# First norm's shift and scale formed on TensorE in column groups, weights loaded by rows

## The reference, cut to what matters

```
mod = c @ w_ada + b_ada                       # 1024 x 6144 weights, 25 MB
sh1, sc1, g1, sh2, sc2, g2 = split(mod, 6)
h    = rms_norm(x, g) * (1 + sc1) + sh1
proj = h @ w_in                               # 1024 x 3080: conv gates | z | xBC | dt (8 columns)
y_a  = short_conv(...); y_b = ssd(...)        # dt = softplus(dt_raw + bias) feeds the decay terms
x    = x + g1 * (concat(y_a, y_b) @ w_out)
h    = rms_norm(x) * (1 + sc2) + sh2
x    = x + g2 * moe(h)                        # 64 experts, top 8, 3 MB of weights each, plus a shared one
out  = rms_norm(x)
```

## Time and profile before

| | |
|---|---|
| three runs, median (lowest to highest) | 707.49 us (707.42 to 708.46) |
| the profiled execution: its time, its span | 708.67 us, 706.9 us |
| PE busy, DVE busy, ACT busy | 642.9, 293.1, 130.7 us |
| DMA, mean over the span | 355 GB/s |

### The profile page before, as it was taken

How to read it: one execution, slowest core, us unless ns; L and a number is a source line. 1 busy time by engine, 2 the same in 40 slices (tenths; PEclk the granted TensorE clock), 3 DMA queues, 4 the chain that set the end, 5 groups by cost and what they waited for, 6 DMA issues and landing times.

```text
span 706.9 us, 11349 instructions
## 1 busy us (share of the span) xinstructions
PE 642.9 (91%) x4206; PEld 374.9 (53%) x4206; DVE 293.1 (41%) x775; ACT 130.7 (18%) x278; POOL 43.4 (6%) x223
## 2 busy tenths in 40 slices
PE   0469999999998899999999999999999999997882
PEld 0448886854544555556545565455554555553440
DVE  4649996778274233231332313323233232331115
ACT  3501123031320111111111111111111111111112
POOL 7000000000201000000000000000000000000000
PEclk9999999999999999999999999999999999999997
DMA  7998699724029999999999999999999999999951
GB/s 232 395 386 313 246 353 373 292 108 178 1 86 424 420 421 421 419 421 420 420 421 418 423 420 420 422 420 422 420 419 420 420 420 420 421 420 420 420 228 61
DMA packets 46010, 250.72 MB, mean 355 GB/s; under 512 B 4673, under 2 KB 7809, under 8 KB 20993
## 3 DMA queue, kind: packets, MB, share of 16 engines
q1 hardware_dynamic: 44434, 248.59, 86.6%
q10 hardware_dynamic: 1520, 1.39, 0.6%
HBM read 248.91 MB, written 1.05 MB: 354 GB/s over the span
## 4 chain that ended last, share of the span: by engine, by line
PE 67%; DVE 17%; DMA 12%; issue 1%; ACT 1%; ACTq 1%; SPq 0%; DVEq 0%
PE PS L1529 10%; PE PS L1525 9%; PE PS L1535 9%; PE PS L1508 8%; DVE MOD L871 7%; DMA ring<-in_we_up_dram 7%; PE PS L1583 5%; DMA ring<-in_w_ada_dram 5%; PE PS L1561 5%; PE PS L1557 5%; PE PS L1566 4%; PE PS L1579 2%; PE PS L1544 2%; PE PS L1325 1%; PE PS L1471 1%
## 5 line engine op out<-in xcount | busy, mean ns | idle before, releaser
L1167 DVE SCALAR_TENSOR_TENSOR arena<-arena,gate,PS 128x128 f32<-128x128 f32 (+1 forms) x48 | 17.9, 373 | 176.6 <-ACT arena L786 176.6
L1529 PE MATMUL PS<-ring,arena 128*64 128x256 f32 x736 | 88.4, 391 | 0.0
L1325 PE MATMUL PS<-hT,ring 128*128 128x256 f32 x384 | 84.8, 380 | 0.0
L1325 PEld LDWEIGHTS PS<-hT,ring 128*128 128x128 f32 x384 | 72.5, 190 | 11.1 <-issue 1.6
L1178 DVE TENSOR_TENSOR YLO<-PS,YHI 128x512 fp32r<-128x512 f32 x57 | 39.4, 691 | 93.3 <-ACT YHI L797 93.3
L871 DVE SCALAR_TENSOR_TENSOR MOD<-ring,ccol,MOD 128x768 f32<-128x768 f32 (+2 forms) x72 | 66.9, 930 | 13.1 <-ACT MOD L664 6.7
L1535 PE MATMUL PS<-ring,arena 128*32 128x256 f32 x1024 | 64.4, 403 | 7.5 <-DMA ring<-in_we_up_dram 7.5
L1508 PE MATMUL PS<-G,H2HI 128*128 128x256 f32 (+1 forms) x256 | 69.5, 307 | 1.3 <-ACT arena L777 0.7
L1525 PE MATMUL PS<-ring,arena 128*128 128x512 f32 x144 | 66.4, 612 | 0.6 <-issue 0.6
L1529 PEld LDWEIGHTS PS<-ring,arena 128*64 128x64 f32 x736 | 49.6, 134 | 31.7 <-issue 2.1
L797 ACT CAST YHI<-PS 128x512 fp32r<-128x512 f32 x57 | 33.5, 587 | 169.3 <-PE PS L1561 79.7
(11 more groups left out here) (255 smaller groups left out, 623.5 us busy)
## 6 DMA issues: line engine op xcount, KB each, us to landing
ring<-in_we_gate_dram SPq DMA_DIRECT2D x64, 1024.0 KB, 18.1
ring<-in_we_up_dram SPq DMA_DIRECT2D x64, 1024.0 KB, 20.7
ring<-in_we_down_dram SPq DMA_DIRECT2D x64, 1024.0 KB, 19.3
ring<-in_w_ada_dram SPq DMA_DIRECT2D x5, 3072.0 KB, 11.4
ring<-in_w_in_dram SPq DMA_DIRECT2D x3, 3072.0 KB, 18.0
ring<-in_w_ada_dram SPq DMA_DIRECT2D x4, 1536.0 KB, 15.8
ring<-in_w_out_dram SPq DMA_DIRECT2D x1, 3072.0 KB, 18.7
ring<-in_w_ada_dram SPq DMA_DIRECT2D x1, 2048.0 KB, 26.0
```

What stands on the lines that cost most here:

```text
L1325: mm = pe.matmul(PS[:, 2 + q % QB, 0:TOK], w[:, k, (m % 6) * P:(m % 6) * P + P], hT[:, k, :], start=(k == 0), stop=(k == KD - 1))
L1529: m = pe.matmul(PS[64 * c:64 * c + 64, 6, 0:FE].rearrange("p (a n) -> p a n", a=2), xt[:, k, :], gu_cols(w[0], k, c), start=(k == 0), stop ...
```

## The change

- The first 2048 columns of `w_ada` come in three pieces by rows (3, 3 and 2 of the 8 row groups, all 2048 columns, `ADA_K`), and PE forms c times them itself (`ada_rows`): per row group four matmuls, one for each group of 32 array columns, each with c repeated 32 times as weights and 512 columns moving. DVE adds the bias once (`mod1`), and four matmuls turn the result into columns. DVE's `ada(0)`, `ada(1)` and `ada(2)` are gone.
- The other 4096 columns come in six pieces, again 2048 columns wide and 3, 3 and 2 row groups; DVE's `ada(3)` to `ada(8)` do one instruction of 2048 columns per row group. One piece more stands in `LOADS`, and `w_in` piece 2 now stands ahead of the first of these six.
- `mod_rows` 0 to 3 need three of the six pieces, rows 4 to 7 all six. Rows 4 and 5 move behind group (0, 0) of the out projection.
- Applying `AB1` to `hT` is shared: even k on DVE, odd k on ACT. The dt matmuls use four column groups; a matmul with `lastcols` sums the groups and picks the eight dt columns.
- The bias is no longer copied by ACT from a row in the ring: four broadcasts of 64 KB and one row of 16 KB are loaded on ACT's queue. ACT's loads of the router weights and gains (WR, gffn, gfin, 1.25 MB) now stand behind its part of `hT`.

```diff
-LOADS = [(A, 0, 0), (A, 1, 1), (A, 2, 2), (I, 3, 3), (A, 3, 1), (I, 2, 0), (A, 4, 2), (I, 1, 1), (A, 5, 2),
-         (I, 0, 3), (A, 6, 2), (O, 0, 0), (S, 0, 1), (A, 7, 2), (O, 1, 3)]
+LOADS = [(A, 0, 0), (A, 1, 1), (A, 2, 2), (I, 3, 3), (I, 2, 0), (A, 3, 1), (A, 4, 2), (I, 1, 1), (A, 5, 2),
+         (I, 0, 3), (A, 6, 2), (O, 0, 0), (A, 7, 2), (S, 0, 1), (A, 8, 2), (O, 1, 3)]
+ADA_COLS = 2 * D
+ADA_K = [(0, 3), (3, 6), (6, 8)]
@@ def _(sp):
-                    user[s] = (ada_acc, nada)
+                    user[s] = (ada_used, j + 1) if j < 3 else (ada_acc, j - 2)
+                    c0, (k0, k1) = ADA_COLS * (j // 3), ADA_K[j % 3]
+                    sp.dma_start(ada_w(n), w_ada[0, :, c0:c0 + ADA_COLS].rearrange("(p k) n -> p k n", p=P)[:, k0:k1, :]
+                                 ).then_inc(loaded[s], 16)
@@ def _(act):
+            for g in range(4):
+                act.dma_start(bias1[32 * g:32 * g + 32, :],
+                              b_ada[0, 512 * g:512 * g + 512].partition_broadcast(32)).then_inc(bias1_in, 16)
+            act.wait_ge(mod_zero, 1)
+            act.dma_start(MOD[0:1, 2 * D:6 * D], b_ada[0:1, 2 * D:6 * D]).then_inc(bada_in, 16)
...
+            act.wait_ge(ab1_ready, 1)
+            act.wait_ge(xnT_ready, 4)
+            for k in range(1, KD, 2):
+                act.activation(hT[:, k, :], hT[:, k, :], ACT.Identity, bias=AB1[:, KD + k:KD + k + 1],
+                               scale=AB1[:, k:k + 1]).then_inc(h1_odd, 1)
@@ def _(dve):
+                k0, k1 = ADA_K[j % 3]
+                dve.wait_ge(loaded[slot_of(n)], loaded_count(n))
+                dst = MOD[:, ADA_COLS * (j // 3):ADA_COLS * (j // 3) + ADA_COLS]
+                for k in range(k0, k1):
+                    ins = dve.scalar_tensor_tensor(out=dst, in0=w[:, k - k0, :], scalar=ccol[:, k:k + 1], in1=dst,
+                                                   op0=ALU.mult, op1=ALU.add)
+                    link(ins, ada_acc if k == k1 - 1 else None)
...
+            dve.wait_ge(ada_used, 3)
+            dve.tensor_tensor(mod1, bank(1), bias1, ALU.add).then_inc(mod1_ready, 1)
...
-            ada(2)
             ada(3)
+            ada(4)
             for b in CONVS[0:3]:
                 conv(b)
-            ada(4)
+            ada(5)
@@ def _(pe):
+            def ada_rows(part_no):
+                n = load_no(A, part_no)
...
+                for k in range(k0, k1):
+                    for g in range(4):
+                        m = pe.matmul(PS[32 * g:32 * g + 32, 1, :], ccol[:, k:k + 1].to_broadcast([P, 32]),
+                                      ada_w(n)[:, k - k0, 512 * g:512 * g + 512], start=(k == 0), stop=(k == KD - 1))
+                m.then_inc(ada_used, 1)
...
+            for q in range(4):
+                m = pe.matmul(PS[:, 0, q:2 * KD:4], mod1[:, q * P:(q + 1) * P], ident[:, 0:P:32], start=True, stop=True)
...
             def mod_rows(r):
-                pe.wait_ge(ada_acc, (c0 + 512 + PIECE - 1) // PIECE)
+                pe.wait_ge(ada_acc, 3 * (r // 4 + 1))
...
-            for r in range(6):
+            for r in range(4):
                 mod_rows(r)
...
                     m.then_inc(mix_ps, 1)
+                    if (t, h) == (0, 0):
+                        for r in range(4, 6):
+                            mod_rows(r)
```

More of the change, by code:

```diff
@@ L257, in build @@
         x_in = sem("x_in")
-        ada_half = [sem(f"ada{j}_half") for j in range(2)]
-        ada2_first = sem("ada2_first")
-        ada2_used = sem("ada2_used")
+        ada_used = sem("ada_used")
+        mod1_ready = sem("mod1_ready")
+        bias1_in = sem("bias1_in")
         in3_late = sem("in3_late")
@@ L284, in build @@
         h1_ready = sem("h1_ready")
+        h1_odd = sem("h1_odd")
+        ab1_ready = sem("ab1_ready")
         dtrow_ps = sem("dtrow_ps")
@@ L850, in link, with ada @@
                 dve.wait_ge(s, signal(ins, s))
-            dve.memset(MOD[:, 0:2 * D], 0.0).then_inc(mod_zero, 1)
-            def ada(j, first_columns=False):
+            def ada(j):
                 n = load_no(A, j)
                 w = ada_w(n)
[L857 to L871, removed]
-                                                   op0=ALU.mult, op1=ALU.add)
[L873 to L878, removed]
+                k0, k1 = ADA_K[j % 3]
[3 more added lines that the diff above has]
+                    ins = dve.scalar_tensor_tensor(out=dst, in0=w[:, k - k0, :], scalar=ccol[:, k:k + 1], in1=dst,
+                                                   op0=ALU.mult, op1=ALU.add)
+                    link(ins, ada_acc if k == k1 - 1 else None)
             dve.wait_ge(ss_ready, TT)
@@ L884, in _ @@
             dve.wait_ge(small_in, 16 * 5)
-            ada(1)
-            ada(2, first_columns=True)
+            dve.wait_ge(bias1_in, 16 * 4)
+            dve.wait_ge(ada_used, 3)
+            dve.tensor_tensor(mod1, bank(1), bias1, ALU.add).then_inc(mod1_ready, 1)
             dve.wait_ge(modcol_ps, 1)
@@ L951, in _ @@
                 conv(b)
-            ada(5)
+            ada(6)
             dve.wait_ge(xsT_ps, 1)
@@ L993, in _ @@
                                              ALU.mult), wts_ready)
-            ada(6)
+            ada(7)
             dve.wait_ge(y_ps, 1)
@@ L1023, in _ @@
                 signal(dve.tensor_tensor(YC[:, b, :], YC[:, b, :], CB[:, b, :], ALU.mult), ya_ready)
-            ada(7)
+            ada(8)
             dve.wait_ge(modrow_ready, 2)
@@ L1283, in _ @@
             pe.transpose(PS[:, 7, 0:R_END], prm, ident[0:R_END, 0:R_END]).then_inc(prm_ps, 1)
+            def ada_rows(part_no):
+                n = load_no(A, part_no)
+                k0, k1 = ADA_K[part_no]
+                pe.wait_ge(loaded[slot_of(n)], loaded_count(n))
+                for k in range(k0, k1):
[3 more added lines that the diff above has]
+                m.then_inc(ada_used, 1)
+            pe.wait_ge(ccol_in, 16)
+            ada_rows(0)
+            ada_rows(1)
             pe.wait_ge(xn_ready, TT)
@@ L1289, in _ @@
             m.then_inc(xnT_ps, 1)
-            for j in range(2 * KD):
-                if j * P < 2 * PIECE:
-                    pe.wait_ge(ada_acc, j * P // PIECE + 1)
-                else:
-                    pe.wait_ge(ada2_used, 1)
-                m = pe.matmul(PS[:, 0, j:j + 1], MOD[:, j * P:(j + 1) * P], ones[:, 0:1], start=True, stop=True)
+            ada_rows(2)
+            pe.wait_ge(mod1_ready, 1)
+            for q in range(4):
+                m = pe.matmul(PS[:, 0, q:2 * KD:4], mod1[:, q * P:(q + 1) * P], ident[:, 0:P:32], start=True, stop=True)
             m.then_inc(modcol_ps, 1)
@@ L1381, in _ @@
                 if q == 0:
[L1382 removed]
+                    dt_cols()
                 if q == 5:
```

67 lines of the change are left out of this document (28 added, 39 removed).

## The result

The changed kernel takes 713.72 us, the median of four runs (712.56 to 715.73). The kernel before, run beside it, takes 707.54 (707.42 to 708.46, four runs). The ratio is 1.0088, with a 95% interval from 1.0059 to 1.0116: the change makes the kernel slower by 6.2 us. The forecast was 713.9. The profiled execution after took 715.73 us with a span of 714.0, where the one before took 708.67 with 706.9. The other three runs of after had spans of 713.0, 710.9 and 710.8.

The account below looks back on a forecast made before the run. The expert stretch, a load stream of fixed length starting when the router is done, was taken as the bound. +2.0 at L1351, -0.8 before L1376 and +5.2 at the new wait gave 707.49 + 6.4 = 713.9 us, range 706.8 to 717.5.

Parts of the forecast that it names:

- What bounds the kernel: Expert stretch: a load stream of fixed length from the router's end; whatever comes before moves the end by as much.
- The front of the kernel: Start up to the projections: they start at 41 instead of 49, 8 us sooner, bounds 39.5 to 43.
- What DVE waits for: Dense stretch: DVE's first of six w_ada pieces lands at 60.5, last Silu ends 99.2, PE waits 8.7 us before the transposes.
- The clock, twice: PE's slowed clock behind two waits: 1.6 us lost after the transposes' wait, 1.5 us after the wait for ada(8).
- The rival in which the clock does not fall at the second wait: Wait for ada(8): waits as predicted but no clock loss there, 712.4 us; counted inside the main case, 0.70 in all.
- Late at L1351's twin: Behind the transposes and two projection blocks: L1351 starts at 108.9 instead of 106.90, 2.0 us late.
- The middle: L1351 to the out projection: PE regains 0.8 us before L1376, 1.2 late; out projection starts at 153.1.
- The new wait: Behind out projection group (0, 0): PE waits 3.7 us for ada(8), plus 1.5 for the clock, +5.2 us.
- The faster one: Early loads at 421 GB/s: first of DVE's six pieces before about 54.5, front's gain kept, 705.3 us at best; chance 0.11.
- the one without change: First of DVE's six pieces lands at 55 to 56, gain and loss cancel, 707.5 us; chance 0.07.
- the later one: First of DVE's six pieces lands at 63, plus a wait for piece 6: 717.5 us; chance 0.12.
- The sum: Residual sum onward: +2.0 at L1351, -0.8 before L1376, +5.2 at the wait for ada(8), 6.4 us late.

Follow-up runs that it names:

- e8: e7 with w_out's last part ahead of piece 8 of w_ada in the load order; 697.73 us, ratio 0.9864 to the kernel before.
- e6: e5 plus DTX ahead of ada(6), ada(6) in ada(7)'s place, ada(7) and ada(8) together ahead of the residual sum, broadcasts as in e1; 720.87 us, ratio 1.0191.
- e4: Changed kernel with the first of DVE's six w_ada pieces loaded ahead of w_in piece 2 again; 712.2 us, ratio 1.0065.
- e5: Changed kernel with three convolutions ahead of ada(3) and ada(5) moved behind all eight convolutions on DVE; 716.22 us, ratio 1.0106.
- e2: Changed kernel with four unused matmuls filling PE's wait ahead of the row 4 broadcast; 710.64 us, ratio 1.0042.
- e7: e6 with ada(7) between y sums and reciprocal, w_ada pieces 7 and 8 in slot 1, shared and first experts' slots changed to suit; 703.67 us, ratio 0.9941.
- e1: Changed kernel with the broadcasts of rows 4 and 5 behind group (0, 1) of the out projection instead of (0, 0); 707.12 us, ratio 0.9991.
- e3: e2 plus ten unused matmuls in PE's wait ahead of the transposes of the convolved part; 709.91 us, ratio 1.0041.

## Why the prediction was right, step by step

**What bounds the kernel.** Right. In all profiled kernels the end follows the first expert load to within 1.2 us: +6.9 and +7.1 in after, -11.6 and -11.5 in e8 (span 695.4 for 706.9); furthest off is e6, +13.5 and +12.3.

**The front of the kernel.** Right in substance, 3 us off in size: I had the projections at 41, they start at 37.97. About 2.5 of the 3 are the loads: the last of the first pieces landed near 30.5, not 33. The rest of the sum, 7.7, measured 7.5, with two errors that nearly cancel: the four matmuls that make columns took 1.05 and not 1.87, and dt_raw took 2.63 and not 1.5, at a granted clock of 0.50 from 35 to 38 us. The sag between 8 and 18 us is the cause, as the next rows show. The window's packets in after, and its windows up to the first piece for DVE:

```profile
DMA packets 1198, 3.61 MB, mean 361 GB/s; under 512 B 631, under 2 KB 631, under 8 KB 887
...
0.00:58.43 58.43, 38.41 (x201) 24.67 (x202) 8.99 (x32) 14.82 (x26) 13.55 (x93) 0.91 0.98 368
```

The tiny packets of ACT's loads are still there, but the rate is 361 GB/s instead of 252. The queues' own rows for this stretch have 774 packets of SP's queue beside 766 of ACT's before, and 598 beside 599 after: one for one. While they alternate, what SP's queue moves depends on the size of its packets, 3.2 KB then (2.50 MB) and 6.0 KB now (3.59 MB). Before, from 18 to 30 us, when ACT's queue had only 161 packets left beside 1829, packets of 2.6 KB moved at 400 GB/s, so it is not their size alone. I had the stretch "gone as well" as the bound of 57 for piece 3, and argued in the rivals that the tiny packets were still there. They were, and did less harm. That the larger rows are the cause is read from these counts alone; no run has the old rows with the new program. The bytes were right: 368 GB/s over 58.43 us are the 21.5 MB of the sum.

**What DVE waits for.** Right, with the whole chain shifted by that load. Piece 3 at 58.43 (60.5 predicted, bounds 57 to 63), `ada(4)` from 65.79 to 72.9, three instructions of 2048 columns 7.13 us and two 4.74 (7.2 and 4.8), a wait of 2.96 before `ada(5)` (2.6), the last Silu's end 97.19 (99.2), PE's wait 9.34 (8.7). e4 and e5 confirm the reason: PE's early start does not matter, since DVE's order and the stream of loads set the Silu.

**The clock, twice.** The mechanism is right, the size was half of what it should be: 1.6 and 1.5 us predicted, 3.0 and 2.9 measured in the profiled execution; e2 gave 3.1 back for the second. My price came from one row, 1.7 us behind an idle time of 2.96 us. There the clock was low for some 3.7 us, here PE worked at 0.50 for some 6 us. The earlier trace rows had a second price that I did not use: 5.99 us for the 16 instructions of L1305, where 16 of L1325 with the same 256 columns took 3.72, so 2.3 us were lost there. Each took 631 ns on the median, L1325's 379, as L1330's take 634 in after at a granted clock of 0.50 and 379 at 1.00. (The clock row of before reads 1.00 for that stretch; the durations contradict it, and so they do in after before 18 us, where 24 instructions of L1280 took 5.25 us and 16 later ones 1.92.) The other runs give 1.7 us behind a wait of 11.12 (e5, 3.60 for 1.88), 1.5 behind 7.39 (e7, 15.48 for e1's 14.00) and 2.9 behind 24.67 (e6, 16.91 for 14.00): between 1.5 and 3.0, and not by the length of the wait. The rival in which the clock does not fall at the second wait is out. The Trainium skill ("TensorE: Matmul & The Clock Gate", Part 1) gives two levels for a core that computes alone, 1.2 and 2.4 GHz; a mean of 0.75 over 3.8 us is then time at both. The trace agrees: its 1 us windows have 0.50 and then 1.00. The Trainium skill also calls the number of slow matmuls "run-variable". The traces agree: the first wait cost 3.0 us in after and 2.6 in e2, where nothing ahead of it was changed.

**Late at L1351's twin.** +2.0 predicted, +1.1 measured: 2.0 less by the earlier Silu, 1.1 more by the clock and what hangs on it. e3 adds what I had not seen: without the clock loss PE gains only part of its 3 us, for the most part because DTX isn't ready.

**The middle.** "1.2 late" was wrong: 0.0. Of that, 0.9 is the first term. I had then taken PE's 0.82 us of slack off, which would leave 0.3 late. The slack was more than 0.82: behind a wait PE's next group also shows 0.1 us longer (1.98 for 1.88 at L1351, 1.99 for 1.89 at L1376), and the group ahead of it is 7.17 long, where without a wait the next one starts 7.01 behind its start. That the out projection then starts 0.4 early, not late, is due to the two broadcasts fewer: I had them at nothing because of the load of `w_out`. It is issued at 146.57 (146.63 before) and is waited for (1.34 us), but before it was the broadcasts that set the start, up to 152.05.

**The new wait.** Right in place and kind: PE idle 3.53 us (3.7), then the broadcasts, group (0, 1) and DVE's two steps. +5.2 predicted; from -0.4 at the out projection to +6.6 at L1027 it is 7.0. Of the 1.8 more, 1.4 is the clock and 0.4 the head start of the out projection, which `ada(8)`, beginning at 157.66 as before, took back. e1 puts it beyond doubt: the two broadcasts one group later give back 6.6 us.

**The rivals.** The faster one needed piece 3 by 54.5, the one without change at 55 to 56, the later one at 63; it landed at 58.43. The first had a right mechanism in it, a milder sag with larger rows, but it brought 2 of its 7 us. The late one's wait for piece 6 was 1.19 us, up to 97.83, about what the sum itself had.

**The sum.** 6.4 predicted for L1027, 6.6 measured. The closeness is partly luck: the loads came 2 us sooner and the middle kept nothing, and both clock terms were too small by 1.4. The errors cancelled. The same holds for the median: the profiled execution moved by 7.1 us, the median by 6.2, and the forecast of 6.4 lies between.

**Left open.** The 3 us between the four runs of after (spans of 710.8 to 714.0) can't be placed, since only one of them was profiled. That e2 has no such spread (0.45 us) would point to the second wait, but e1, without that wait, has 2.9 us, and the kernel before 2.9 over 16 runs. The same holds for e5's one run of 711.88.

## What to carry to other kernels

When a change makes one engine faster ahead of a meeting point, look for what the other side of each following meeting stands behind: here PE's 11 us went into a wait for DVE, DVE's 10 us into a wait for a load, and the version was 9 us faster only when convolutions, DTX, two broadcasts, two pieces and one load had changed places. Moving one of them alone (e5) only moved the wait. A wait put into an in-order engine or queue costs what is queued behind it (6.6 us for two broadcasts, 24.67 us for one load), so price the queue, not the instruction. And price an idle time of PE of 3 us or more with its clock: here 1.5 to 3.0 us on top. Whether that reaches the end of the program depends on the other side again (3.0 us of clock at the first wait, 0.7 of time).

## What the runs showed of the hardware

- Behind idle times of 3.53 and 9.34 us TensorE's granted clock was 0.50 for some 6 us of work, then 1.00. The loss was 2.9 us after the short one and 3.0 after the long one; behind 7.39 (e7), 11.12 (e5) and 24.67 us (e6) it was 1.5, 1.7 and 2.9, so it did not follow the length of the idle time. Ordinary matmuls without use, issued in the wait, kept the clock up (1.99 us for the broadcasts instead of 3.78, 7.07 for two projection blocks instead of 9.18).
- The clock row can read 1.00 early in a trace while the durations say otherwise: 631 ns for 256 columns at L1305 before, 379 at L1325. At a granted clock of 0.50, 256 columns took 634 ns in after.
- Loads of two queues took turns packet by packet: 774 beside 766, and 598 beside 599. A queue with next to no bytes in it (0.01 MB in 599 packets) went with a rate of the other that followed its bytes per packet: 252 GB/s with 3.2 KB packets, 361 with 6.0 KB.
